# The delta rule of a four-mixer block: keys and queries left unnormalized, gates by tokens, and all eight turns written out

## The reference

```python
q = l2norm(q) * DK ** -0.5          # l2norm(x) = x * rsqrt(sum(x * x) + EPS)
k = l2norm(k)                       # q, k, v: silu of a causal convolution over 4 tokens
beta = sigmoid(b_raw)
g = -exp(a_log) * softplus(a_raw + dt_bias)
g = cumsum(g)                       # within a chunk; decay = exp(g_i - g_j)
L = strict_lower((k * beta) @ k.T * decay)
u, w = solve(I + L, [v * beta, k * beta * exp(g)])
attn = lower(q @ k.T * decay)
for each chunk:
    v_new = u - w @ state
    o = (q * exp(g)) @ state + attn @ v_new
    state = state * exp(g_last) + (k * exp(g_last - g)).T @ v_new
y = (rmsnorm(o, norm_g) * silu(gate)) @ w_out
```

## Time and profile before

| | |
|---|---|
| median of 3 runs | 2838.11 us |
| profiled execution, its own time | 2837.48 us |
| span of its trace | 2835.6 us |
| PE busy | 2666.6 us, 94% |
| DVE, ACT, POOL busy | 1585.9, 1055.5, 1126.3 us |
| mean granted clock of PE | 0.974 |
| HBM | 69 GB/s over the span |

### The profile page before, as it was taken

The page is one execution under the profiler, slowest core; times in us unless marked ns, Lnnn a source line. Parts: engine busy times, 40 slices in busy tenths (PEclk is TensorE's granted clock), DMA queues, the critical chain, the costliest instruction groups (busy, mean ns, idle before and its releaser), DMA issues.

```text
span 2835.6 us, 34373 instructions
## 1 busy us (share of the span) xinstructions
PE 2666.6 (94%) x12110; PEld 2066.6 (73%) x12110; DVE 1585.9 (56%) x2682; ACT 1055.5 (37%) x1500; POOL 1126.3 (40%) x1445
## 2 busy tenths in 40 slices
PE   8999979999999789999999899998999997989996
PEld 6888758888888657777777678886887766756663
DVE  5655465556656533344444455554988963356565
ACT  3222343333333343333333232224345664435543
POOL 4666433323233124333333346664554424423320
PEclk9999989999999999999999999999999998999997
DMA  3223211111111112122212212222222111211110
GB/s 126 97 97 99 89 64 60 48 56 44 59 59 38 52 43 67 62 67 67 68 62 68 75 68 97 90 97 83 97 97 67 64 48 60 96 38 60 66 38 30
DMA packets 57085, 195.71 MB, mean 69 GB/s; under 512 B 6416, under 2 KB 8976, under 8 KB 56976
## 3 DMA queue, kind: packets, MB, share of 16 engines
q1 hardware_dynamic: 55824, 192.90, 20.5%
q10 hardware_dynamic: 1152, 1.38, 0.2%
HBM read 192.15 MB, written 2.10 MB: 69 GB/s over the span
## 4 chain that ended last, share of the span: by engine, by line
PE 86%; DVE 8%; ACT 3%; issue 2%; DMA 0%; SPq 0%; POOL 0%; ACTq 0%; DVEq 0%
PE psum L310 22%; PE psum L312 22%; PE psum L311 22%; PE psum L1708 4%; PE psum L2314 1%; PE psum L2284 1%; DVE psum L884 1%; PE psum L423 1%; PE psum L2287 1%; PE psum L1714 1%; PE psum L2627 1%; PE psum L2656 1%; PE psum L1777 1%; ACT whi L276 1%; PE psum L2308 1%
## 5 line engine op out<-in xcount | busy, mean ns | idle before, releaser
L291 POOL TENSOR_TENSOR wlo<-raw,whi 128x256 fp32r<-128x256 f32 x1436 | 1125.9, 816 | 1646.7 <-ACT whi L276 1646.7
L310 PE MATMUL psum<-xh,whi 128*128 128x512 f32 x1832 | 763.1, 417 | 19.9 <-DVE xl L404 7.3
L311 PE MATMUL psum<-xl,whi 128*128 128x512 f32 x1832 | 718.6, 392 | 0.0
L312 PE MATMUL psum<-xh,wlo 128*128 128x512 f32 x1832 | 718.5, 392 | 0.0
L276 ACT ACTIVATE whi<-raw 128x1024 fp32r<-128x1024 f32 (+1 forms) x367 | 377.3, 1036 | 832.1 <-PE psum L312 831.5
L310 PEld LDWEIGHTS psum<-xh,whi 128*128 128x128 f32 x1832 | 347.3, 190 | 102.5 <-issue 30.7
L311 PEld LDWEIGHTS psum<-xl,whi 128*128 128x128 f32 x1832 | 347.7, 190 | 75.3 <-issue 11.3
L312 PEld LDWEIGHTS psum<-xh,wlo 128*128 128x128 f32 x1832 | 346.4, 189 | 75.1
L482 DVE TENSOR_TENSOR xT<-psum,xT 128x512 f32<-128x512 f32 x192 | 130.8, 688 | 197.3 <-PE psum L312 197.3
L310 PE MATMUL psum<-pool_yh,whi 128*128 128x512 f32 x256 | 102.5, 400 | 0.0
L311 PE MATMUL psum<-pool_yl,whi 128*128 128x512 f32 x256 | 101.7, 397 | 0.0
(11 more groups left out here) (508 smaller groups left out, 4592.4 us busy)
## 6 DMA issues: line engine op xcount, KB each, us to landing
raw<-weights_dram SPq DMA_DIRECT2D x335, 512.0 KB, 3.3
raw<-weights_dram SPq DMA_DIRECT2D x32, 384.0 KB, 2.9
xin<-x_dram SPq DMA_DIRECT2D x4, 512.0 KB, 6.6
out_dram<-y SPq DMA_DIRECT2D x4, 512.0 KB, 2.6
g_masks<-gdn_masks_dram ACTq DMA_DIRECT2D x1, 384.0 KB, 3.2
par<-params_dram SPq DMA_DIRECT2D x1, 319.5 KB, 2.9
mwork<-positions_dram ACTq DMA_DIRECT2D x1, 256.0 KB, 2.9
o_pT<-positions_dram ACTq DMA_DIRECT2D x1, 256.0 KB, 2.9
```

Source lines behind the costliest of these rows:

```text
L291: last = pool.tensor_tensor(wlo[:, q, part], raw[:, q, part], whi[:, q, part].bitcast(F32), ALU.subtract)
L310: pe.matmul(gbank(b), whi[:, q, c:c + P], h, start=k == 0, stop=False)
L311: pe.matmul(gbank(b), whi[:, q, c:c + P], l, start=False, stop=False)
L312: done = pe.matmul(gbank(b), wlo[:, q, c:c + P], h, start=False, stop=k == nk - 1)
```

## The change

- k and q are not normalized. k's factor goes into the columns that multiply k by k (`cE`), the states' products (`cS`) and v (`cV`); ACT sums the squares of k along the transposed tokens with `accum_out`. q's factor cancels in the outputs' norm but for epsilon: the squares of q, scaled, are added to those of the outputs. The sums over k and q squares and `normalize` go.
- Gates are formed by tokens: 128 partitions by 32 columns (chunk and head). Prefix sums become a product with a triangle of ones.
- The row of G is picked by a one-column fp32r factor from 40 rows (high and low parts).
- N2 and N4 transposed are four transposes each, and ACT takes them out of the bank. "w" goes: the state is multiplied by k itself (kS), DVE subtracts that from v beta (rhs), and U is applied to the result.
- The loop goes. All turns are written out, and turn i now itself computes v and the output gate of head i, then k and q of head i+1, then the output tiles of head i-1. `PIECES` says how many pieces stand at each of PE's places, `TAKES` how many side steps of DVE (intakes, taps, adds) at each of its own. Before turn 0 stand only the tiles of the gates, k and q. The weights come in the new order.

```diff
-            stg = sb("stg", [P, 4, SEQ])
-            qn, kn, vs = stg[:, 0, :], stg[:, 1, :], stg[:, 2:4, :]
-            rqk = sb("rqk", [P, 2, SEQ])
...
+            kb = sb("g_k", [P, 2, SEQ])
+            qv = sb("g_qv", [P, 3, SEQ])
             kdec = sb("kdec", [P, NCH, P])
+            kkc = sb("kkc", [P, NCH, P])
...
+                z, e, u, r, q, is0, eb, t = (gts[:, a, :] for a in range(8))
...
+                dve.tensor_tensor(zrow[:, :], bank(BA)[0:16, :], R[0:16, :], ALU.mult).then_inc(*taken(S, BA, 0))
...
-                dve.reciprocal(Q[b8, :], tmp[2][b8]).then_inc(*vbs.done("beta"))
...
+                dve.reciprocal(gcol[:, 0, :, :].rearrange("p c h -> p (c h)"), eb).then_inc(*ve.done("beta"))
...
-            def normalize(dve, h):
-
-                dve.tensor_scalar(Gm[:, :], Q[a8, :], ident[a8, ds(h + 32, 1)] if not isinstance(h, int) else
-                                  ident[a8, 32 + h:33 + h], None, ALU.mult).then_inc(*vp.done("G masked"))
-                for x, name in ((1, "k"), (0, "q")):
-                    dve.wait_ge(*ap_.at(f"1/norm {name}", h))
-                    dve.tensor_tensor(stg[:, x, :], stg[:, x, :], rqk[:, x, :], ALU.mult)\
-                       .then_inc(*vp.done(f"{name} normed"))
...
+            def q_square(act, i):
+                if i:
+                    act.wait_ge(*ve.of(f"{i - 1} o summed"))
+                act.wait_ge(*ae.of(f"{i} silu {QQ}"))
+                act.activation(qsq, stream(QQ, i), ACT.Square, scale=math.sqrt(DV * 128 * EPS))\
+                   .then_inc(*ae.done(f"{i} q square"))
...
-                pe.wait_ge(*vp.at("G masked", i))
-                pe.matmul(wbank(3), ones[0:8, :], Gm[:, :], start=True, stop=True).then_inc(*te.done("G row"))
...
+                pe.wait_ge(*ae.of(f"{i} silu {K}"))
+                pe.wait_ge(*(ve.of(f"{i - 1} y gated 1") if i else ve.of("rows")))
+                four_transposes(0, kc, "k tokens")
+                pe.matmul(wbank(3), pick[:, i:i + 1].to_broadcast([40, P]), Ghl[:, :], start=True, stop=True)\
+                  .then_inc(*te.done(f"{i} G row"))
+                four(2, kc, kc, "kk")
+                more("kk")
+                pe.wait_ge(*ve.of(f"{i} N"))
+                four_transposes(0, N, "N transposed")
+                more("N transposed")
+                pe.wait_ge(*ve.of(f"{i} Nt"))
+                four(2, NB[:, 0], N, "N2")
+                pe.wait_ge(*ae.of(f"{i} silu {QQ}"))
+                pe.wait_ge(*ae.of(f"{i} exp G row"))
+                four(3, kc, qc, "kq")
+                more("N2")
+                pe.wait_ge(*ve.of(f"{i} N2"))
+                four_transposes(0, NA[:, 0], "N2 transposed")
+                if i:
+                    pe.wait_ge(*ae.of(f"{i - 1} ln o"))
...
+                four(1, NA[:, 0], U, "U2")
+                more("U2")
+                pe.wait_ge(*ae.of(f"{i} N2 transposed"))
+                four(2, NA[:, 1], NA[:, 0], "N4")
+                more("N4")
+                pe.wait_ge(*ae.of(f"{i} N4"))
+                four_transposes(0, NB[:, 0], "N4 transposed")
+                pe.wait_ge(*ve.of(f"{i} U2"))
+                four(1, NB[:, 0], U, "U4")
+                more("U4")
+                pe.wait_ge(*ae.of(f"{i} N4 transposed"))
...
-                pe.wait_ge(*ve.at("U join 2", i))
-                four(0, kbe, U, "w")
...
+                    if s == 1:
+                        pe.wait_ge(*ae.of(f"{i} silu {V1}"))
+                        pe.wait_ge(*ve.of(f"{i} A"))
+                        v_tokens(0)
+                pe.wait_ge(*ve.of(f"{i} v beta 0"))
+                v_tokens(1)
+                pe.wait_ge(*ve.of(f"{i} U join 2"))
                 for c in range(NCH):
...
+                        pe.matmul(wbank(1)[:, 0:DV], kc[:, c, :], St[:, (c - 1) % 2, :], start=True, stop=True)\
+                          .then_inc(*te.done(f"{i} kS {c}"))
+                        if c == 1:
+                            pe.wait_ge(*ve.of(f"{i} q exp G"))
                         for d in range(2):
-                            pe.matmul(wbank(2 + d)[:, c * P:(c + 1) * P], S[:, (c - 1) % 2, d * P:(d + 1) * P],
+                            pe.matmul(wbank(2 + d)[:, c * P:(c + 1) * P], St[:, (c - 1) % 2, d * P:(d + 1) * P],
                                       chunks(eg[:, :])[:, c, :], start=True, stop=False)
-                        more(1)
-                        pe.wait_ge(*ve.at(f"v new {c}", i))
...
+                pe.wait_ge(*ve.of(f"{i} o summed"))
+                pe.matmul(wbank(1), ones, osq[:, 0, :], start=True, stop=True).then_inc(*te.done(f"{i} o sum"))
...
+                act.wait_ge(*te.of(f"{i} k tokens"))
+                for c in range(NCH):
+                    last = act.activation(ksq[:, c * P:(c + 1) * P], wbank(0)[:, c * P:(c + 1) * P], ACT.Square,
+                                          accum_out=ssk[:, c:c + 1])
+                last.then_inc(*ae.done(f"{i} k squares"))
...
+                act.wait_ge(*ae.of(f"{i} k squares"))
+                act.activation(rln, ssk, ACT.Ln, bias=bias[:, 0:1]).then_inc(*ae.done(f"{i} ln k"))
+                act.wait_ge(*ae.of(f"{i} ln k"))
+                act.activation(rk, rln, ACT.Exp, scale=-0.5).then_inc(*ae.done(f"{i} 1/norm k"))
+                act.wait_ge(*te.of(f"{i} N2 transposed"))
+                act.activation(NA[:, 1, :, :], chunks(wbank(0)), ACT.Copy).then_inc(*ae.done(f"{i} N2 transposed"))
+                hi_after(act, S, 0, hi[0], True)
...
+                act.wait_ge(*te.of(f"{i} o 3"))
+                for d in range(2):
+                    act.activation(osq[:, d, :], wbank(2 + d), ACT.Square).then_inc(*ae.done(f"{i} o square {d}"))
+                if i < H - 1:
+                    silu(act, K, i + 1)
+                    silu(act, QQ, i + 1)
+                    q_square(act, i + 1)
+                act.wait_ge(*te.of(f"{i} o sum"))
+                act.activation(ro, wbank(1), ACT.Ln, scale=1.0 / DV, bias=bias[:, 5:6]).then_inc(*ae.done(f"{i} ln o"))
+                act.wait_ge(*ae.of(f"{i} ln o"))
+                act.activation(ro, ro, ACT.Exp, scale=-0.5).then_inc(*ae.done(f"{i} 1/rms o"))
+                if i:
+                    hi_after(act, S, 0, hi[-2], True)
+                    hi_after(act, S, 0, hi[-1], True)
...
+                dve.wait_ge(*ae.of(f"{i} k squares"))
+                dve.tensor_scalar(ssk1, ssk, EPS, None, ALU.add).then_inc(*ve.done(f"{i} ss+eps"))
+                dve.wait_ge(*ve.of(f"{i} ss+eps"))
+                dve.reciprocal(r2, ssk1).then_inc(*ve.done(f"{i} 1/ss"))
+                dve.wait_ge(*ve.of(f"{i} 1/ss"))
+                dve.tensor_tensor(cE, r2, beta, ALU.mult).then_inc(*ve.done(f"{i} beta/ss"))
+                dve.wait_ge(*ve.of(f"{i} beta/ss"))
+                dve.wait_ge(*te.of(f"{i} kk"))
+                dve.tensor_tensor(kkc[:, :, :], chunks(wbank(2)), spread(cE), ALU.mult).then_inc(*ve.done(f"{i} kk beta"))
+                dve.wait_ge(*ae.of(f"{i} E2"))
+                dve.tensor_tensor(d2[:, :, :], d2[:, :, :], over(nstrict), ALU.mult).then_inc(*ve.done(f"{i} E2 masked"))
+                if i == 0:
+                    dve.wait_ge(*ae.of("exp last-G"))
+                dve.tensor_tensor(kdec[:, :, :], chunks(wbank(0)), spread(dec), ALU.mult).then_inc(*ve.done(f"{i} k dec"))
+                dve.wait_ge(*ve.of(f"{i} E2 masked"))
+                dve.tensor_tensor(N[:, :, :], kkc[:, :, :], d2[:, :, :], ALU.mult).then_inc(*ve.done(f"{i} N"))
+                dve.tensor_tensor(cS, cE, mexp, ALU.mult).then_inc(*ve.done(f"{i} -beta exp G/ss"))
...
+                        dve.wait_ge(*te.of(f"{i} kS {c}"))
+                        dve.scalar_tensor_tensor(out=vb[:, c, :], in0=wbank(1)[:, 0:DV], scalar=cS[:, c:c + 1],
+                                                 in1=vb[:, c, :], op0=ALU.mult, op1=ALU.add).then_inc(*ve.done(f"{i} rhs {c}"))
+                        fill(f"rhs {c}")
...
+                dve.tensor_tensor(osq[:, 0, :], osq[:, 0, :], qsq, ALU.add).then_inc(*ve.done(f"{i} o half summed"))
+                dve.wait_ge(*ve.of(f"{i} o half summed"))
+                dve.wait_ge(*ae.of(f"{i} o square 1"))
+                dve.tensor_tensor(osq[:, 0, :], osq[:, 0, :], osq[:, 1, :], ALU.add).then_inc(*ve.done(f"{i} o summed"))
...
+            SITES = ["kk", "N transposed", "N2", "U2", "N4", "U4", "N8", "U8", "join 0", "joined 0", "join 1", "joined 1",
+                     "join 2", "joined 2", "v new 0", "o 0", "kS 1", "v new 1", "o 1", "kS 2", "v new 2", "o 2", "kS 3",
+                     "v new 3", "o 3"]
+            PIECES = {0: [7, 2, 2, 1, 2, 1, 2, 1, 2, 1, 2, 1, 2, 1, 2, 1, 2, 2, 2, 2, 2, 2, 1, 1, 4],
+                      H - 1: [8, 2, 2, 1, 1, 2, 1, 1, 1, 1, 1, 1, 1, 1, 1, 1, 1, 1, 1, 1, 1, 1, 1, 1, 4]}
+            PIECES_BETWEEN = [7, 2, 2, 2, 2, 2, 2, 2, 2, 2, 2, 2, 2, 2, 2, 2, 2, 2, 2, 2, 2, 2, 2, 2, 5]
+
```

(32 more changed lines are left out.)

848 lines of the change are left out of this document (407 added, 441 removed).

## The result

The changed kernel takes 2770.63 us (median of 4 runs, 2769.89 to 2776.16) where the kernel before, on the same chip, takes 2837.6 (median of 4). The ratio is 0.9768, 95% interval 0.9751 to 0.9785: 67 us or 2.3% faster. The prediction was 2783.7 us, range 2757 to 2811. The profiled execution after took 2769.89 us, with a span of 2768.1.

What follows compares the result with a forecast made beforehand. The prediction took PE's own work to bound the steady turns. Head, turns, waits and low clock summed to the next layer's first product at 969.1 for 1023.5, so 2838.1 - 54.4 = 2783.7 us, range 2757 to 2811.

Steps and rivals of the forecast that it cites:

- What bounds the kernel: Delta-rule layer: a steady turn of 76.30 us costs what PE has to do in it, PE busy 75.86 of 76 us.
- What a turn loses and gets on PE: Steady turn: products dropped or made cheaper save 5.2 us, less 0.1 each at three places; 76.3 becomes 71.4 us.
- Turns 2 to 6: Five steady turns of 72.6 us each: 0.8 us waiting for N and 0.4 for DVE's side steps booked.
- Head: Layer start through turn 0: turn 0 starts at 370.0 us, idles 2.7 for N, loses 4 to low clock, ends at 436.9.
- Between turn 0 and turn 1: Seam of these turns: PE idles 3.8 us for k, 4.7 for N, with low clock 13 us; the largest loss expected.
- Turn 7: Last turn: 60.2 us of work plus 7.5 of waits, 3 to 4 for replies and about 3.5 at its end.
- The sum: Next layer's first product at 969.1 us for 1023.5: 54.4 us less, so 2783.7 us.
- Steps beside GpSimd: N and the adds of squares, from two SBUF tiles while GpSimd works, are dear; free of it, about 3 us lower.
- Table loads: ACT's chain to N in turn 1: two table loads, around the logarithm, of 1.28 us each.
- The waits don't come: Rival: replies of 0.6 us suffice everywhere, only PE's work remains, 94 us less, half way about 2762; chance 0.17.
- The chain binds each turn: Rival: the longer delta-rule chain keeps turns near 76.3 us, 27 us less gain, 2811; chance 0.16.
- Weights come late: Rival: late weight halves from ACT and GpSimd cost 8.3 us a slot; two a turn give 2917; slower 0.05.

Runs made afterwards that it cites:

- a_lo512: The changed kernel with GpSimd's splitting of the weights in pieces of 512 columns for 256; 2792.42 us (one run).
- a_kk8: The changed kernel with one projection piece moved in turns 1 to 6 from the turn's end to its first place; 2768.75 us.
- the second profile: The changed kernel measured and profiled once more, unaltered; 2773.65 us (median of 5 runs).
- a_early_k: The changed kernel with turn 0's output squares before a weight's high half, key taps before the wait for outputs, one piece moved in turns 1 to 6; 2765.3 us.
- a_slot3: The changed kernel with the gates' weight tile put back from ring slot 0 to slot 3; 2780.51 us, ratio to before 0.9796.
- a_bare7: The changed kernel with turn 7's pieces taken from between its dependent products, 24 piled at its first place; turn 7 86.4 us for 67.8.

## Why the prediction was right, and where it was off

**What bounds the kernel.** Right, and shown by the doubled N8: what PE gets to do in a steady turn is paid in full.

**What a turn loses and gets on PE.** The term was 4.9 us; it is 6.4 (76.30 less 69.9). I added the pitches of all rows of one turn by line, before (566.53 to 642.83) and after (583.31 to 654.02):

| term | booked | found |
|---|---|---|
| sums over k and q squares | 1.7 | 1.7 |
| one sum over output squares | 0.9 | 1.3 |
| row of G | 0.75 | 0.6 |
| N2, N4 transposed | 0.96 | 1.0 |
| "w" | 0.89 | 0.9 |
| more switches of data type | -0.3 | 0 |
| products that stay: recurrence, k by k and q, others | 0 | 0.8 |

The last two are the mis-sized ones. They add up to 6.3, and the 0.1 that is missing is PE's idle time and rounding. The recurrence has as many products as before and takes 6.1 us for 6.7. What makes it cheaper wasn't tried. For the row of G I had no row of its shape; 0.43 lies nearer to the 0.3 taken than to the bound of 1.05.

**Turns 2 to 6.** 72.6 booked, 70.71 found, 1.9 us less, five times. Of that 1.5 us is the term above. The rest is the waits: 1.2 booked, 0.77 found, all of it before N. So the 0.8 booked for N is right, and the 0.4 for DVE's side steps is the part that never came: no wait shows there. N came 7.5 us after the k transposes (583.31 to 590.82), against the 7.3 of the prediction, but by another path than the one named there. The prediction let N follow from ACT's k squares. DVE and ACT in this turn:

```profile
584.38 0.69 DVE L1899 TENSOR_TENSOR d<-psum,gcol 128x512 f32<-128x512 f32 x1 [0.17 <-PE psum L1757]
...
585.44 0.22 ACT L1845 ACTIVATION_READ_ACCUMULATOR sq<-psum 128x1 f32 x1
...
586.85 0.70 DVE L1905 TENSOR_SCALAR g_small<-g_small 128x4 f32<-128x4 f32 x1
...
590.08 0.68 DVE L1919 TENSOR_TENSOR N<-kkc,d 128x512 f32<-128x512 f32 x1
```

The last square is read at 585.66, and the first step that needs it (L1905) starts at 586.85, when DVE has ended what stands before it. From the row of G (L1757) on, DVE has ten steps in a row without idle time, and N is the last. Four of them lie beside GpSimd and take 1.7 us more than without it: 0.93, 0.86, 0.70 and 0.44 us for 0.43, 0.43, 0.17 and 0.17 in turn 1 (L1901, L1903, L1905, L1909). a_lo512 confirms it: with pieces of 512 columns N comes 8.2 us after the k transposes, and PE waits 1.30 us for it. So in a steady turn the wait for N is DVE's own order and its waits for GpSimd; that its size was booked right is luck. In turn 1, where DVE does wait for the squares (4.87 us before L1905), their price counts, and it was booked too high:

```profile
445.09 0.26 ACT L1845 ACTIVATE sq<-psum 128x128 f32<-128x128 f32 x1
...
445.25 0.19 ACT L1845 ACTIVATION_READ_ACCUMULATOR sq<-psum 128x1 f32 x1
445.34 0.27 ACT L1845 ACTIVATE sq<-psum 128x128 f32<-128x128 f32 x1
```

One comes every 0.25 us: the read of the sum (0.19) overlaps with its neighbours, so four cost 1.0 us, not 2.2, and the rows of the attention don't add up as I added them.

**Head.** The step held, its size was 2.2 us short. From the layer's start to turn 0 are 28.0 us for 25.8, of which PE waits 6.0 in four places (1.02, 1.35, 1.48, 2.18). The gates' small steps were booked at 0.1 to 0.2 us and take 0.65 where GpSimd works (0.19 where it doesn't). Turn 0 itself came out at 70.9 for 70.7 by two errors that cancel: N was waited for 0.36 us instead of 2.7, and the wait of 3.69 us for ACT's queue was in no step. That wait is the clearest omission: I had counted the squares from PE's last output product and looked at DVE's queue for what stands ahead of them, and not at ACT's. N was not early: its transposes come 10.4 us after those of k, for 9.2 booked. The wait is short because PE works at a clock of 0.66 over 366 to 376 us; in a_kk8, with 0.83 there, it is 2.05 us.

**Between turn 0 and turn 1.** Its mechanism is shown, its start is not as booked. The k transposes were released by ACT's silu behind DVE's taps, as said, after 2.14 us (3.09 and 3.52 in other runs) for 3.8. But the 3.69 us before the o sum come first: from PE's last output product to the k transposes are 11.4 us (425.70 to 437.09) where k was to be ready after 7.4. N was waited for 1.83 and, in the second profile, 3.22 us for 4.7; the cheaper squares account for 1.2. The clock is 0.50 over 436 to 442 us, in between. a_early_k shows the first link: with the taps done earlier the wait for k is 0.29, and silu no longer ends it. Turn 1 lasts 75.5 and 78.4 us in two profiles for 80.6.

**Turn 7.** 67.7 booked, 67.8 found. PE's busy time is 61.3 for 60.2, the waits 6.5 for 7.5: 4.07 for y (3.5 booked), 2.4 for replies (3 to 4). That it fits to 0.1 us is partly luck. By the steady turn's pitches its work is 58.7 us (69.9 less 16 pieces of 0.7), 1.5 less than booked, and what it loses between its steps is so much more.

**The sum.** From forecast to result in the layer, 17 us: start 6.0 earlier, turn 1 5.1 shorter, turns 2 to 6 9.5 shorter; head, turns 0 and 7 and last products 3.6 longer. So 6 of the 17 us, the start, were in no step of the prediction and have nothing to do with its subject. Of the 71.4 us the run keeps 67. In the profiles the attention's first wait is 8.11 us where it was 6.77:

```profile
961.42 3.54 POOL L291 TENSOR_TENSOR wlo<-raw,whi 128x256 fp32r<-128x256 f32 x5
...
964.21 0.84 DVE L2217 CAST maskb<-cst 128x128 bf16<-128x128 f32 x1 [8.28 <-ACT R L440]
...
974.34 2.08 PE L2285 MATMUL psum<-sq,cst 128*128 128x512 f32 x2 [8.11 <-ACT sq L2271]
```

The cast takes 0.84 us and ends with GpSimd's pieces; in a_slot3, where no GpSimd piece lies beside it, it takes 0.23, and the wait is 6.77. That is 0.6 of the 1.3 us; the other 0.7 I can't place. The remaining 2.5 us, from the attention's first product to the end, lie within what one execution scatters (below).

**Steps beside GpSimd.** The prediction feared the price of the normalizing product for N and for the adds of squares, 3 us. It shows in the traces: before, the 14 normalizing products of heads 1 to 7 take 1.22 to 1.25 us, all beside GpSimd's pieces (head 0's two take 0.78 and 1.21), while q times exp(G), of the same width and also with both inputs in SBUF, takes 0.68 with no piece beside it (L1873). After, the same step takes 1.12, beside pieces (L1943). But the medians of N and the adds are 0.68 and 0.69 us (one add of 16 took 1.10), so the 3 us stayed away; in the turn shown, GpSimd's pieces end at 588.92, before N is made. The cost appeared elsewhere: the taps of q and v take 0.90 us on average for 0.75 of before, and the small steps and the two before them 1.7 us in N's chain. **Table loads:** in the chain at 441 us a load starts at 441.26 and the next ACTIVATE at 442.55, so a switch is 1.29 us where 1.28 was booked.

**The rivals.** "The waits don't come" was put at about 2762 (half of 40 from 2783.7 is 2764), and that lies nearer to 2770.6 than my 2783.7 does. In the steady turns it was nearer too; at the seam of turns 0 and 1 it was wrong. "The chain binds each turn" is out: 70.71 us. "Weights come late" shows nowhere in the layer of the changed kernel (the one wait for GpSimd at the layer's start even went), though a_bare7 shows how near it is: 4.65 us as soon as PE uses its pieces in a block.
